# Down weights of a mixture of experts in 8 KB pieces, with the activations transposed by every second column

## The reference

```python
def expert_block(args):
    xb, e = args
    return (jax.nn.silu(xb @ w_g[e]) * (xb @ w_u[e])) @ w_d[e]
```

## Time and profile before

| | |
|---|---|
| median of 3 runs | 1450.2 us (1447.04 to 1451.2) |
| the profiled execution | 1449.73 us, with a span of 1447.5 us |
| mean granted TensorE clock | 0.974 |
| TensorE busy | 1337.3 us, 92% of the span |
| VectorE, ScalarE, GpSimd busy | 442.9, 244.9, 187.5 us |
| DMA | 435.78 MB in 93090 packets |

### The profile page before, as it was taken

One profiled execution on the slowest core, in us unless ns is written; L12 is line 12 of the kernel. 1 busy time (PEld: TensorE's weight loads), 2 busy tenths in 40 slices (PEclk: granted clock), 3 DMA queues, 4 the chain that ended last, 5 costly groups with the idle time before them and its releaser, 6 DMA issues.

```text
span 1447.5 us, 17576 instructions
## 1 busy us (share of the span) xinstructions
PE 1337.3 (92%) x5883; PEld 581.9 (40%) x5883; DVE 442.9 (31%) x882; ACT 244.9 (17%) x478; POOL 187.5 (13%) x244
## 2 busy tenths in 40 slices
PE   5999987989979999999999999999999999999992
PEld 4878765744453333333333333333333333333330
DVE  4799454532234221121121112112112112111214
ACT  3132545740110000000000000000000000000002
POOL 3354432100000001001001001000100100100100
PEclk9999998999989999999999999999999999999996
DMA  5332210134345999999999999999999999999954
GB/s 200 111 117 69 106 58 1 60 116 157 133 175 217 376 405 413 410 397 411 406 409 399 399 414 395 405 407 402 391 416 411 400 402 407 399 404 413 414 239 178
DMA packets 93090, 435.78 MB, mean 301 GB/s; under 512 B 13488, under 2 KB 13517, under 8 KB 60810
## 3 DMA queue, kind: packets, MB, share of 16 engines
q1 hardware_dynamic: 86896, 429.23, 74.7%
q0 software_dynamic: 5312, 5.28, 1.1%
q10 hardware_dynamic: 858, 0.95, 0.2%
HBM read 429.10 MB, written 18.36 MB: 309 GB/s over the span
## 4 chain that ended last, share of the span: by engine, by line
issue 78%; PE 12%; DVE 3%; POOL 2%; DMA 2%; ACT 1%; POOLq 1%; ACTq 0%; DVEq 0%
PE ps_proj L1186 9%; PE ps_proj L1227 2%; POOL sb_tick L577 1%; POOL sb_tick L588 1%; DVE sb_x L1135 1%; DMA sb_weights<-in_w_in 1%; DMA sb_rb_sb<-in_rel_bias 1%; ACT sb_scratch L684 1%; PE ps_scores L1241 0%; DVE sb_scratch L893 0%; PE ps_proj L1209 0%; POOL expert_rows L578 0%; DVE sb_scratch L896 0%; DVE sb_x L1145 0%; POOL sb_weights_r L556 0%
## 5 line engine op out<-in xcount | busy, mean ns | idle before, releaser
L1398 PE MATMUL ps_proj<-sb_weights,sb_scratch 128*64 128x512 f32 x1984 | 446.9, 592 | 0.8 <-DVE sb_scratch L1100 0.8
L1419 PE MATMUL ps_scores<-sb_weights,sb_scratch 128*64 128x512 f32 x992 | 240.2, 605 | 29.3 <-ACT sb_scratch L763 29.3
L1398 PEld LDWEIGHTS ps_proj<-sb_weights,sb_scratch 128*64 128x64 f32 x1984 | 142.3, 137 | 283.2 <-issue 282.1
L1375 PE MATMUL ps_proj<-sb_hT,sb_scratch 128*64 128x512 f32 x1008 | 240.1, 598 | 0.0
L1110 DVE TENSOR_TENSOR sb_scratch<-sb_scratch,ps_proj 128x256 f32<-128x256 f32 x62 | 26.1, 421 | 589.1 <-ACT sb_scratch L761 589.1
L577 POOL TENSOR_TENSOR sb_tick<-sb_tick 1x1 f32<-1x1 f32 x62 | 11.7, 188 | 1041.1 <-ACT sb_scratch L769 1041.1
L1186 PE MATMUL ps_proj<-sb_hT_r,sb_weights_r 128*128 128x512 f32 x512 | 131.5, 412 | 2.9 <-POOL sb_weights_r L556 2.9
L1375 PEld LDWEIGHTS ps_proj<-sb_hT,sb_scratch 128*64 128x64 f32 x1008 | 72.9, 138 | 145.6 <-issue 145.6
L761 ACT ACTIVATE sb_scratch<-ps_proj 128x256 f32<-128x256 f32 x62 | 23.8, 384 | 545.0 <-PE ps_proj L1398 545.0
L1186 PEld LDWEIGHTS ps_proj<-sb_hT_r,sb_weights_r 128*128 128x128 f32 x512 | 100.3, 199 | 32.8 <-issue 11.1
L1419 PEld LDWEIGHTS ps_scores<-sb_weights,sb_scratch 128*64 128x64 f32 x992 | 60.2, 136 | 125.3 <-issue 81.2
(11 more groups left out here) (217 smaller groups left out, 858.5 us busy)
## 6 DMA issues: line engine op xcount, KB each, us to landing
sb_weights<-in_w_exp_down SPq DMA_DIRECT2D x124, 1024.0 KB, 9.4
sb_weights<-in_w_exp_gate SPq DMA_DIRECT2D x124, 1024.0 KB, 8.8
sb_weights<-in_w_exp_up SPq DMA_DIRECT2D x124, 1024.0 KB, 10.7
sb_weights<-in_w_in SPq DMA_DIRECT2D x9, 2048.0 KB, 8.2
sb_x<-in_x SPq DMA_DIRECT2D x8, 512.0 KB, 8.9
sb_weights<-in_w_out SPq DMA_DIRECT2D x2, 2048.0 KB, 10.2
sb_weights<-expert_rows SPq DMA_DIRECT2D x4, 1024.0 KB, 8.0
sb_weights<-in_w_conv_pw SPq DMA_DIRECT2D x1, 2048.0 KB, 7.7
```

Source lines behind the costliest of these rows:

```text
L1375: last = mm(ps_rows[g * BLK:(g + 1) * BLK, :], onehot[:, t, :], h2[:, t, g * NW:(g + 1) * NW], start=t == 0, stop=t == T - 1)
L1398: last = mm(ps_gu[g * BLK:(g + 1) * BLK, :].rearrange("p (a n) -> p a n", a=2), hTb[:, c, half * BLK:(half + 1) * BLK], weights[:, place(p ...
L1419: last = mm(ps_y[g * BLK:(g + 1) * BLK, :], actT[:, j, half * BLK:(half + 1) * BLK], weights[:, place(parity, 4 + half), 2 * j + g, :], st ...
```

## The change

The source of a down sixth is read by another pattern: a partition p gets the rows 256 h + 2p and 256 h + 2p + 1, which are adjacent, so 8 KB in one piece. In `weights` row j of the two still lies in the places 2j and 2j + 1, and the matmuls at L1419 read the same places as before. To match, transpose j takes the columns j, j + 2, j + 4 and so on of `act`, so that partition p of `actT` holds inner column 2p + j. No instruction is added, removed or moved on any engine. From the second edit on, line numbers are one higher than before.

```diff
         act = scratch[:, 2304:2560]
+        act_jf = act.rearrange("p (f j) -> p j f", j=2)
...
-            wd = ap("w_exp_down")[0].rearrange("e (h j p) n -> e h p j n", h=2, p=P)
+            wd = ap("w_exp_down")[0].rearrange("e (h p j) n -> e h p (j n)", h=2, p=P)
...
                 else:
-                    dst = dst.rearrange("p a (j q) n -> p (a j) (q n)", j=2)
-                    src = wd[e, i - 4].rearrange("e p j n -> (e p) j n")
+                    dst = dst.rearrange("p a b n -> p (a b n)")
+                    src = wd[e, i - 4].rearrange("e p n -> (e p) n")
                 sp.dma_start(dst, src).then_inc(in_w[i], 16)
...
                 for c in range(2):
-                    last = pe.transpose(ps_actT[:, c * P:(c + 1) * P], act[:, c * P:(c + 1) * P], ident)
+                    last = pe.transpose(ps_actT[:, c * P:(c + 1) * P], act_jf[:, c, :], ident)
                 last.then_inc(actT_done, 1)
```

## The result

The changed kernel takes 1453.37 us in the median of 20 runs (1449.25 to 1456.26), the kernel before 1449.38 us in as many. The ratio is 1.0027, with a 95% interval of 1.0018 to 1.0036: some 4 us slower. (One of the 20 runs before took 3341.65 us, and the ratio leaves it out.) The forecast was no change, 1450 us. The measured time lies in the range given and inside the 0.3% that I had called no change, but 20 runs tell a difference of 0.27% from none, and it is a loss.

A forecast was written before the change was run, and what follows sets the result against it. The prediction took TensorE to bound the loop, with transfers covered. Its terms, 0 from the transfers, 0 from SP and 0 from the transposes, on a median of 1450.2 us gave 1450 us, range 1446.5 to 1455 us.

The forecast's parts named there:

- What bounds the loop: Loop over expert blocks: TensorE sets the pace, waiting 29.3 us for ACT's copy and never for a DMA.
- Part 1, the transfers: Down-weight transfers in 8 KB pieces: up to 1.0 us a block saved beside TensorE's work, 0 on the path.
- Part 2, the transposes: The two transposes a block reading every second column: on the path without cover, cost taken as 0, bounded by +27 us.
- the upper end: Transpose pair at half rate: a full doubling adds 0.44 us a block, 27 us in all.
- The rival of the strided read: Strided reading slows the transposes in 62 blocks; 17 us with both weight loads doubled, 1467 us; chance 0.08.
- It decides from 0.07 us a block: Strided-read cost in the transposes from which the time would differ from no change, 4.3 us over 62 blocks.
- The rule on 16-byte lines: SBUF reads need two hits per 16-byte line for full rate; the transposes' 8-byte step gives two, so cost nil.
- Transfers as the bound: Rival: transfers pace the loop, so down weights save up to 1.0 us a block, 60 us in all; chance 0.04.
- Signs: Trace marks named beforehand: if right, 15.68 us a block and 140 ns transpose load; if wrong, a pair above 0.44 us.
- the sum: Whole kernel: 0 from the transfers, 0 from SP's issues, 0 from the transposes, giving 1450 us.

The follow-up runs named there:

- e1: Changed kernel with the old transposes of adjacent columns, so only the 8 KB down pieces are new: 1448.51 us, ratio 1.0004.
- d1: g1 (4 KB down pieces) with half of the gather of the next block's rows left out: 1412.56 us, ratio 0.9772.
- d2: d1's gather edits on the changed kernel with adjacent-column transposes and VectorE's product reading with an 8-byte step: 1405.79 us, ratio 0.9724.
- e2: Kernel before (4 KB down pieces) with the new transposes of every second column: 1452.31 us, ratio 1.0032.
- e8: Kernel before with only the first of the two transposes reading every second column: 1451.79 us in one run.
- e6: Kernel before with transposes reading every fourth column (16-byte step): 1454.35 us in one run.
- e7: Kernel before with transposes reading every third column (12-byte step): 1450.58 us in one run.
- g1: Kernel before with a quarter of the next block's gather moved behind the transposes, filling TensorE's wait for ScalarE's copy: 1418.07 us, ratio 0.9785.

## Why the prediction was wrong, point by point

- **What bounds the loop.** Right. TensorE's waits were 29.3 us for ScalarE and none for a DMA, and with the new transfers alone nothing changed (e1).
- **Part 1, the transfers.** Right at 0 on the path. The bound of up to 1.0 us a block was ten times too large: where transfers do set the pace, they save 0.09 us (d1, d2). It came of taking 350 and 416 GB/s from two windows of a few us as the rates of the two kinds of piece. The traces show that neither was such a rate. The 4 us window in the same phase of 56 blocks (from 11.1 us ahead of the transposes) has 342 to 421 GB/s before the change, 394 in the mean, so the 350 was one of the three lowest; after it, with the down weights in 8 KB pieces, it has 338 to 422, 395 in the mean. The later phase has 419 and 417. So about two thirds of the difference was the chance of one window. The phase does have a dip, but it is the same with either size of piece. In d1, which has 4 KB pieces, the dip is gone (417 GB/s in the same phase). This points to supply: before the change SP issues nothing for up to 5.0 us while it waits for the down products, and in d1 it seldom waits for TensorE. Supply was not tried by itself. A rate should be read from many blocks, and from a stretch in which the transfers are the bound.
- **Part 2, the transposes.** Wrong, and this is the step of the prediction that failed: "I take 0, because the instruction reads the same elements and only every second word is skipped". An equal number of elements did not take an equal time: the weight load took 207 ns for 140, and 206 ns in e2, where the step is all that changed. The place was named rightly (on the path in 62 blocks, no cover) and the cost bounded from both sides, 0 to 27 us; the value was set at the lower end with no row for it. The measured 0.068 us a block, 4.2 us in all, is a sixth of the upper end.
- **The rival of the strided read** was the right one, at a chance of 0.08, too low for a cost that no row excluded and that nothing would have covered. Its price of 17 us took both loads as doubled. The load grew by half and did not double, and the second is nearly hidden behind the first pass (e8), which makes 4 us of 17. "It decides from 0.07 us a block" was where the result came out.
- **The rule on 16-byte lines** that the prediction cites made the cost nil at this step. The measurement decides against it for this load (e2, e6, e7).
- **Transfers as the bound** did not come about, and by d1 and d2 the gain would have been some 6 us, not 60, had they been.
- **Signs.** Right: packets fewer by 15871, TensorE's waits of 29.4 us for L764 alone. Down landings came 1.4 us sooner, a little more than said. Wrong: period 15.75 us, passes 335 ns, load 207 ns. The sign of being wrong that was named, a pair longer than 0.44 us with a later copy behind it, is what came: 0.50 us. SP's two down issues took 1.03 us together, not 0.7, which cost nothing.

The range held the time, but only because the rival had been given a share of it; the sum itself had no term for the loss.

## What to carry to other kernels

An access pattern with a step is not free because it reads as many elements: ask which instruction reads or writes it, and how many such instructions stand on the path. Here the same reordering cost 4 us in the transposes' weight load, 11 us in a scattered write of VectorE, 21 us in the moving operand of the large products, and nothing as a strided read of VectorE. And larger pieces paid nothing here as long as TensorE set the pace: its idle time had to be filled first (g1, 30 us), after which the transfers ran at 415 to 418 GB/s and their landings took 13 to 15 us instead of 9 to 11.

## What the runs showed that I had not expected

- A float32 weight load of 128 columns, in these pairs of transposes, takes 141 ns with adjacent columns and 200 to 207 ns with a step of 2, 3 or 4 words, hardly depending on which. The first load of a pair alone takes 138 and 190 to 197 ns.
- A matmul record of 512 columns takes about 11 ns longer when its moving operand has a step of 2 words in runs of 128, far less for each column than the load.
- VectorE's product of 256 columns reads SBUF and PSUM with a step of 8 bytes in the same 421 ns as without, and takes 603 ns when it writes neighbours 512 bytes apart.
- A loop that is paced by transfers moves 415 GB/s with a third of its bytes in 4 KB pieces and 418 GB/s with all weights in 8 KB pieces.
